# Mixer front of a two-block transformer kernel: operations reordered, and its last stage split by token tile

## The reference, cut to what matters

```
z = rmsnorm(h, g_mix) @ w_in                      # conv val/gate, rwkv inputs, two gates
y_a = conformer_conv(conv_val, conv_gate, ...)    # 31 taps, layer norm, silu, @ w_conv_out
y_b = rwkv7_mix(rwkv_in, ...)                     # 8 heads of 64: a delta-rule scan over time,
                                                  # group norm, bonus, times g, @ w_rwkv_out
h = h + (gate_a * y_a + gate_b * y_b) @ w_o
x = rmsnorm(h, g_ffn); q = x @ w_q; s = q . sub_keys      # 8 heads x 2 halves x 128 keys
e, gate = top 16 of the 16 x 16 sums of the best keys     # per token and head
h = h + sum_e gate * gelu(x . expert_u[e]) * expert_v[e]  # 128 experts per token
```

## Time and profile before

| | before |
|---|---|
| median of 3 runs (range) | 2632.99 us (2631.33 to 2634.02) |
| the profiled execution: its time | 2636.66 us |
| its span | 2634.9 us |
| busy: TensorE, VectorE, ScalarE, GpSimd | 2310.8, 1664.3, 909.2, 881.1 us |
| share of the span in which TensorE was busy | 88% |
| bytes moved | 951.79 MB, of them 805.36 MB by the gathers |
| granted clock of TensorE, mean | 0.970 |

### The profile page before, as it was taken

The page is one execution under the profiler, slowest core; times in us unless marked ns, Lnnn a source line. Parts: engine busy times, 40 slices in busy tenths (PEclk is TensorE's granted clock), DMA queues, the critical chain, the costliest instruction groups (busy, mean ns, idle before and its releaser), DMA issues.

```text
span 2634.9 us, 27740 instructions
## 1 busy us (share of the span) xinstructions
PE 2310.8 (88%) x8722; PEld 1321.6 (50%) x8722; DVE 1664.3 (63%) x3961; ACT 909.2 (35%) x2671; POOL 881.1 (33%) x804
## 2 busy tenths in 40 slices
PE   7989988888988989989899889988889999987776
PEld 6889855444445543545544545434545435532322
DVE  2864136666667677566677576767576866676764
ACT  2232003233324443234343333534234524333232
POOL 0013003334343334333334333343333343344432
PEclk9999689999999999999999999999999999999999
DMA  5420037999999999999999999999999999999996
GB/s 184 132 80 1 25 103 305 421 421 421 421 422 419 418 418 392 421 421 421 421 406 409 421 421 421 422 421 397 421 417 417 396 421 417 421 405 421 421 421 285
DMA packets 154451, 951.79 MB, mean 361 GB/s; under 512 B 17178, under 2 KB 19626, under 8 KB 55876
## 3 DMA queue, kind: packets, MB, share of 16 engines
q0 software_dynamic: 110592, 805.36, 73.8%
q1 hardware_dynamic: 43716, 144.69, 14.5%
HBM read 948.93 MB, written 1.05 MB: 361 GB/s over the span
## 4 chain that ended last, share of the span: by engine, by line
DMA 45%; PE 37%; DVE 9%; ACT 5%; issue 3%; POOL 1%; DVEq 0%; ACTq 0%; POOLq 0%
DMA arena<-in_uv,idx 45%; PE bank L1545 19%; PE bank L347 7%; DVE arena L1566 5%; PE bank L581 1%; ACT arena L1603 1%; PE bank L717 1%; PE bank L734 1%; PE bank L567 1%; PE bank L1307 1%; ACT arena L1591 1%; POOL arena L1619 1%; ACT arena L1597 1%; PE bank L541 1%; PE bank L1217 0%
## 5 line engine op out<-in xcount | busy, mean ns | idle before, releaser
L1545 PE MATMUL bank<-arena 128*128 128x512 f32 x3072 | 1445.8, 616 | 274.2 <-ACT arena L1603 270.7
L1619 POOL DMA_INDIRECT arena<-in_uv,idx x768 | 846.2, 1102 | 1515.6 <-PE bank L1545 1309.7
L1545 PEld LDWEIGHTS bank<-arena 128*128 128x128 f32 x3072 | 571.0, 195 | 1002.5 <-issue 591.4
L1566 DVE CUSTOM_DVE_ANT_0 arena<-arena,h 128x1024 f32<-128x1024 f32 x512 | 627.5, 1226 | 439.7 <-DMA arena<-in_uv,idx 436.9
L1591 ACT ACTIVATE arena<-arena 128x2 f32<-128x2 f32 x384 | 78.2, 204 | 1273.9 <-DVE arena L1566 1273.4
L1566 DVE CUSTOM_DVE_ANT_0 arena<-arena 128x1024 f32<-128x1024 f32 x256 | 313.8, 1226 | 231.3 <-DMA arena<-in_uv,idx 230.3
L347 PEld LDWEIGHTS bank<-xT,weights 128*128 128x128 f32 x2528 | 351.2, 193 | 70.2 <-issue 47.7
L347 PE MATMUL bank<-xT,weights 128*128 128x128 f32 (+2 forms) x2528 | 378.0, 305 | 0.9 <-ACT xT L782 0.9
L1603 ACT ACTIVATE arena<-const,arena 128x128 f32<-128x128 f32 x768 | 260.4, 386 | 0.0
L1597 ACT ACTIVATE arena<-arena 128x1 f32<-128x1 f32 x768 | 184.8, 288 | 12.6
L1152 POOL TENSOR_TENSOR arena<-arena 128x512 f32<-128x512 f32 (+1 forms) x32 | 34.7, 1109 | 208.5 <-DVE arena L1015 185.0
(11 more groups left out here) (306 smaller groups left out, 1741.5 us busy)
## 6 DMA issues: line engine op xcount, KB each, us to landing
weights<-in_w_q SPq DMA_DIRECT2D x80, 512.0 KB, 8.4
weights<-in_w_in SPq DMA_DIRECT2D x38, 512.0 KB, 3.5
weights<-in_a_fm SPq DMA_DIRECT2D x28, 512.0 KB, 9.1
arena<-in_uv,idx POOLq DMA_INDIRECT x768, 14.5
weights<-in_a_out SPq DMA_DIRECT2D x16, 512.0 KB, 7.8
weights<-in_b_fm SPq DMA_DIRECT2D x16, 512.0 KB, 7.9
weights<-in_b_out SPq DMA_DIRECT2D x16, 512.0 KB, 9.8
weights<-in_a_v SPq DMA_DIRECT2D x16, 384.0 KB, 7.7
```

The source lines that it names most:

```text
L1545: ins = nc.tensor.matmul(acc[:, :], diag[:, e % DIAGS, :], ring[:, e % RING, at:at + 512], start=first, stop=last)
L1566: V.tensor_tensor_reduce(out=u, in0=u, in1=x, scale=1.0, scalar=0.0, op0=ALU.mult, op1=ALU.add, accum_out=dots[:, unit % 2, kx:kx + 1]).th ...
L1619: nc.gpsimd.indirect_dma_start(out=ring[:, s, :], out_offset=None, in_=io[f"uv{unit // PH // NT}"], in_offset=bass.IndirectOffsetOnAxis(ap ...
```

## The change

The same numbers are computed. In the order of the program:

- **Start.** A small Sqrt comes first on ScalarE. ScalarE squares token tile 0 and the meta tokens, VectorE tile 1. The reciprocal roots go into three diagonals (`rdiag`), and a product with them scales and transposes at once, so `hn` is gone. Six products of zeros come first on PE. The first gate tile follows the emptied banks one by one. The two broadcasts of row vectors are issued behind 12 weight blocks.
- **Gates 4 to 6** are emptied ahead of the three Exps.
- **Groups** go meta first. MT and NT of all groups stand before QK and QB, and two parities alternate product by product, each in its own half of the array's rows and its own bank. The first join is ahead of QK's and QB's masks.
- **UA** is one product of 128 columns in place of two of 64, on a side-by-side operand (`RHS`).
- **Chunk sums, states, outputs**: chunks 1 and 2, or the two parities, alternate in the same way. Outputs, group norm and `w_rwkv_out` go token tile by token tile.
- **Gate tiles 10 to 15** are cut into 24 pieces of two products, in banks `acc_lo` and `acc_hi` (`fill`), and spread over UA to the transposes.
- **Bonus** and its factors move to GpSimd; three of VectorE's passes go.
- **`w_o`** has a place of its own in SBUF, as have the six first query blocks. Tile 0's eight row blocks come first, then three of tile 1; then tile 0's norm, head 0 and head 1; then tile 1's other five; then head 2; then tile 1's norm and heads 0 and 1. Tile 1's residual and norm stand on VectorE behind unit 0's top-k. The gather of expert 3 waits for tile 1's `w_o`, and PE's first expert product for its residual.

The core of the diff:

```diff
@@ one_tensor
-            pe.wait_ge(sem("const_in"), 16)
-            pe.wait_ge(sem("hn_ready"), 3)
+            for _ in range(6):
+                nc.tensor.matmul(acc_lo[:, :], flat[:, 0:P], flat[:, P:P + 512], start=True, stop=True)
+            pe.wait_ge(sem("rdiag_ready"), 3)
...
-                nc.tensor.transpose(out[:, META:META + P], hn[:, 0, f], ident)
+                nc.tensor.matmul(out[:, META:META + P], h[:, 0, f], rdiag[:, 0, :], start=True, stop=True)
...
+            for i in ("meta", 0, 1):
+                products((("MT", beta, alpha), ("NT", kappa, alpha)), i)
+            for i in range(NT):
+                products((("QK", kappa, rho), ("QB", beta, rho)), i)
...
-            gate_tile(pe, GATES_AT["NV"])
...
-                    nc.tensor.matmul(out[0:n, m * P:m * P + RH], Wm[g][:, m, :], NV[g][0:n, m, :], start=True, stop=True)
-                    ins = nc.tensor.matmul(out[0:n, m * P + RH:(m + 1) * P], Wm[g][:, m, :], tmv(i, 0)[:, hs],
+                    ins = nc.tensor.matmul(out[0:n, m * P:(m + 1) * P], Wm[g][:, m, :], RHS[i][0:n, par, m, :],
...
+            chunk_reads(0)
+            fill(1)
+            next_state(1)
+            chunk_reads(1)
+            fill(1)
+            next_state(2)
+            fill(1)
+            tile_out(0)
+            next_state(3)
+            fill(2)
+            tile_out(1)
+            fill(6)
+            rwkv_transposed(pe, 0)
+            for _ in gate_pieces:
+                pass
+            rwkv_out(pe, 0)
+            rwkv_transposed(pe, 1)
+            rwkv_out(pe, 1)
...
+            for kc in range(KC):
+                mixed_out(pe, 0, kc, [banks.bank(("w_o", 0, half)) for half in range(2)],
+                          [banks.full_sem(("w_o", 0, half)) for half in range(2)])
+            for kc in range(W_O_FIRST):
+                mixed_out(pe, 1, kc, (acc_lo, acc_hi), None)
@@ one_scalar
+            for j in range(4, 7):
+                gate_in(act, j)
 
             act.wait_ge(sem("cum_ready"), 1)
...
+            fill_in(act, FILL_GATES + 3)
+            group_root(act, 0)
+            rwkv_in(act, 0)
+            for j in range(FILL_GATES + 4, 16):
+                fill_in(act, j)
+            group_root(act, 1)
+            rwkv_in(act, 1)
@@ first_tensor
+            fm_tensor(pe, 0, 0, xn)
+            fm_wait(pe, 0, 0)
+            early_head(0, 0)
+            early_head(1, 0)
+            for kc in range(W_O_FIRST, KC):
+                mixed_out(pe, 1, kc, (acc_lo, acc_hi), None)
+            early_head(2, 0)
+            fm_tensor(pe, 0, 1, xn)
+            fm_wait(pe, 0, 1)
+            early_head(0, 1)
+            early_head(1, 1)
+            yield 0
+            early_head(2, 1)
@@ first_scalar
+            early_head(0, 0)
+            early_head(1, 0)
+            softmax_exp(act, 0)
+            early_head(2, 0)
+            norm_squares(act, 0, 1)
@@ stream_vector
             for _ in range(TOPK_OPS):
                 next(ops)
+            last_residual_in(v)
+            variance(v, 0, 1)
+            first_apply(v, 1)
@@ SyncE
-            at = first["w_q", 0, 0]
-            load_blocks(sp, 0, at)
+            at = first["keys", 0, 0]
+            load_blocks(sp, 0, 2 * SLOTS)
...
+            for par in range(2):
+                sp.wait_ge(*banks.full(("O", 1, par)))
+            for kc in range(KC):
+                sp.dma_start(w_o[:, kc, :], io["w_o"][kc]).then_inc(sem(f"w_o_in_{kc}"), 16)
+            sp.wait_ge(sem("gn_folded"), NT)
+            for j in range(EARLY_Q - 1):
+                sp.dma_start(early_q[:, j, :], io["w_q"][0][j]).then_inc(sem(f"early_q_{j}"), 16)
```

568 lines of the change are left out of this document (334 added, 234 removed).

## The result

Before, on the same chip: 2632.16 us, median of four runs (2629.85 to 2634.02). Changed: **2592.61 us**, median of four (2587.99 to 2596.78). The ratio is 0.985, 95% interval 0.9831 to 0.9869. The profiled execution took 2593.22 us, its span 2591.4, against 2636.66 and 2634.9: 43.4 us less where 45 were forecast. Bytes are the same (951.80 MB), the mean clock 0.976 against 0.970.

A forecast was written before the change was run, and what follows sets the result against it. The expert stream is bound by DMA bytes, so the end follows the first gather plus later idle DMA time. Front -50.9, idle DMA +8.5, query blocks -2.6: net -45, median 2588 us, range 2570 to 2606.

The forecast's parts named there:

- Start: Kernel start to the first full tile: transposes and scaling merged, gate tile begins at about 18.3; -3.3 us (0 to -6).
- products: Products and first level, 176.1 to 199.1: paired row halves, then masks bind, level 1 at +17; -6.1 us.
- outputs to `w_o`: 331.8 to 372.0: gate pieces and token-tile order in place of the group norm wait; -9.2 us (-4 to -12).
- NV and UA: 256.6 to 274.2: gate tile moved elsewhere, UA merged from 9.4 to 4.5 us; -8.3 us.
- Chunk sums to outputs: 274.2 to 331.8: 34 us of work at full clock, clock taken as 0.75; -11.6 us (+8 to -23).
- Switches between products of 128 and 64 rows: Within chunk sums to outputs: 24 more switches, 2 to 6 us, within that term's bounds.
- Behind the first gather: Stream start: first expert product at T+27, ninth gather not before T+30, idle DMA; +8.5 us (2 to 14).
- -2.6 for two query blocks: Two query blocks and their keys, 1.1 MB, land before the first gather instead of after; -2.6 us.
- the covered ramp at the full clock: Rival: everything at full clock, shorter gap behind the first gather; gain 60, 2573 us; chance 0.20.
- The clock staying down: Rival: clock 0.57 from the chunk sums on; gain 28, 2605 us; chance 0.17.
- Pairs did not serialise: Rival: row pairs serialise; products, chunk sums and outputs lose 6 + 3 + 3; gain 33, 2600 us; chance 0.08.
- The idle ring: Rival, slower: full slots idle the DMA until the first expert product, outweighing the gain past 53 us; chance 0.03.

The follow-up runs named there:

- run 7: The changed kernel without the six products of zeros at the start: 2597.87 us.
- run 3: The changed kernel with one gate-tile piece ahead of NV and one between NV and UA, two fewer behind the outputs: 2583.94 us.
- Run 5: The changed kernel with the 24 gate-tile pieces in three places in place of eleven: 2596.07 us.
- Runs 2: The changed kernel with tile 1's transposes and head 0, head 1 and head 2 behind the first, second and third expert products: 2593.17 us.
- 4: The changed kernel with the edits of runs 2 and 3, and tile 1's squares and root ahead of head 2 on ScalarE: 2583.33 us.
- runs 9: Run 3's kernel with ScalarE doing tile 1's squares and root ahead of tile 0's head 2, first two gathers' coefficients ahead of tile 1's head 1: 2570.52 us.
- 10: The changed kernel with run 3's pieces around NV, and tile 1's heads cut up and laid behind the expert products of ten ring steps: 2566.96 us.

## Why the prediction was right, and where it wasn't

2588 was forecast, 2592.6 measured, inside 2570 to 2606; in the profiled executions 45 less was forecast and 43.4 came. That is closer than its parts: the front gained 8.6 us more than forecast, and the stream lost 10.1 us more. That these two cancelled is luck.

- **What bounds the kernel** held throughout: over twelve runs the time follows the first gather plus the idle DMA time behind it. 2233 us from T at 16 us idle, 2224.7 at 8.8, 2214.5 to 2216.8 at 1 to 2.
- **Start, conv output, products, outputs to `w_o`, `w_o`**: -3.6, -4.0, -5.8, -9.3, -8.6 against -3.3, -3.8, -6.1, -9.2, -8.6. The large products took 0.066 us a pass in place of 0.107, not quite the half that I had put; the masks did bind (a wait of 3.52 us for one, then level 1 at +17.2), and the norm of tile 0 was late by 2.45 us. The start's term came near by luck: I had eight groups from 9.5 on at 1.05 us each, and they came from 10.38 on at 0.96 each. The 0.83 us a group that I started from were those of an array at half pace. Without the zeros (run 7) a group takes 1.69 us, and the front would have gained about 5 us less, while the first tile's own 1.5 us were not in my sum. Two more gains that I had at nothing go with the clock: in conv output to products (-1.8) and in the levels (-1.3) the kernel before had 3.4 us at 0.50 each (154.1 to 157.5, behind the wait of 3.81 us, and 198.5 to 201.9), and the changed kernel has none there. No run took back the order of the gates, the merged UA or the group norm by tile alone, so these terms rest on the stretches.
- **NV and UA** (-8.3 forecast, -0.9 measured) is the first step that failed. I took the passes at the price of the full clock, and took the gate tile between them for 3.7 us of movable work. The clock fell inside NV. At the full clock the merged UA takes 5.5 us (run 3, where the next piece starts 5.52 us behind it), against 9.4 before and 4.5 in my sum: its 48 passes are 0.11 us apart, those of the meta tokens too, which I had put at about half. So merging does save passes, but the term was 1 us too large even so, and the rest of what is missing is the clock. The sign stood in the rows I cited: behind the next such stretch, the clock had fallen too.
- **Chunk sums to outputs** (-11.6 forecast, -22.7 measured): the content was right, 34 us, and the assumed clock of 0.75 wrong; it was 1.00. I should have given the rival at the full clock this half. Run 5 shows the cause in part: the pieces fill waits, and behind a wait the clock fell; small products alone kept it for 11 us. Why the same stretch before had 0.62 is only in part explained by it, since TensorE was busy for 54.9 of 57.6 us there.
- **Switches between products of 128 and 64 rows** cost little: with all of them the stretch took 34.8 us, where 34 were summed. Single rows do show a price. In an output step of the changed kernel the 128-row passes come in pairs 0.23 us apart (276.34, 276.57), but the first 64-row pass comes 0.31 us behind the last pair (276.88), and the first pair of the next step takes 0.27 (277.16, then 277.43). That is 0.08 to 0.09 us for the one switch and 0.05 for the other, some 1 us in the eight output steps, the cheaper of the two prices that I had considered. The dearer one, 0.25 us, I had read from the groups at the start, which were slow for the other reason named above. The Trainium skill's rule (TensorEngine Tiling (Array Packing), Key Properties) that a change of tiling mode drains the engine agrees with these rows.
- **Behind the first gather** (+8.5 forecast, 16.1 us idle) is the second step that failed. The first expert product was forecast for T+27 and came at T+31.5: tile 1's transposes started 0.8 us late, and at the half clock they took 1.97 us in place of 1.09 and head 0 6.69 in place of 3.81. And I let the gap end with the ninth gather (T+30), though head 2 of tile 1 stands behind the first pair of products and the eleventh gather waits for the second. That part is 4.4 us of idle time, the larger part of the 7.6 us by which I was short. Runs 2 and 4 show how much it can be: with the first product at T+18 or T+14 and a head behind each pair, 14.6 to 19.2 us were idle all the same. The rule that follows is a rate, not a moment.
- **-2.6 for two query blocks** cannot be told: time from T to the end less idle time is 2218.1 before and 2217.4 after.
- **The rivals**: the covered ramp at the full clock, 2573, did not happen here, but runs 9 and 10 are it (2570.5 and 2567.0). The clock staying down came true for NV and UA alone. Pairs did not serialise. The idle ring never came near the 53 us that it needed.

## What to carry to other kernels

When work is moved from ahead of a DMA-bound stream to behind its start, it is free only if the consumer still frees buffers at the stream's rate: lay it in pieces between the steps (here steps of up to 7.0 us, 5.5 on the mean of ten, for each 5 us of transfers, borne by eight buffers), keep table loads and normalisations of one engine off the path of the first step, and count the rate, not only the first release. A dense independent piece of work can be worth more than its length where TensorE would otherwise stand for a microsecond or run thin products: moving two of 1 us each gave 8.7 us here. And two parts of an estimate that are wrong in opposite ways look like a good forecast; compare the stretches, not the total.

## What the runs showed of the hardware that was not expected

- The clock shown at the start is no witness, because the trace has no clock entry there. Run 7 and the changed kernel both show 1.00 up to 22 us, but the same three products take 1.69 us in one and 0.96 in the other, and the first tile 4.3 and 3.7 us. The pace doubles where the first entry stands: 24.0 us in run 7, 8.0 in the changed kernel, where twelve passes of zeros stood ahead of the groups. In run 9, with a standstill of 0.87 us behind the zeros, the clock fell to 0.50 again from 12.6 to 22.8.
- The clock can fall while TensorE is busy in every microsecond: in NV to UA to 0.50, 1 to 8 us behind the start of NV, in seven of seven profiles without a piece of gate tile there, for 10 to 14 us in six and for 3 in one. The Trainium skill, TensorE: Matmul & The Clock Gate, What's actually happening, ties a throttled clock to idle time; here a standstill of 1.25 us stood ahead of it, and before the change one of 1.04 us had stood at the same place without a fall for 17 us. So idle time of this length is not enough to tell.
- Behind the first gather the changed kernel's clock was 0.50 from 366.4 to 380.1, from just behind a wait of 1.7 us and through one of 5.0. In run 9, where these waits were 0.95 and 0.18 us, it did not fall in the first 90 us of the stream.
- Two row halves overlap also in runs of four products (0.074 us a pass, against 0.066 alternating and 0.107 in runs of sixteen).
